# Attention scores of two steps in one run of half-array matmuls, both causal masks behind them

## The reference, cut to what matters

```
# layer 1: 4 memory heads (256 keys, no mask) and 12 heads of causal attention
#          (96 columns of query and key)
# layer 2: 4 memory heads and 12 causal heads with forget gates:
s = einsum('bqhd,bkhd->bhqk', q_i, k) * scale + (F[t] - F[s])
p = softmax(where(key_pos <= q_pos, s, -inf));  out = p @ v
# layer 3: 16 heads of stick breaking
logits = q[:, q0:kend] @ k[:, :kend].T * scale;  mask = ki < qi
log_fail = where(mask, log_sigmoid(-logits), 0)
between = cumsum(log_fail, reverse) - log_fail
w = where(mask, exp(log_sigmoid(logits) + between), 0);  out = w @ v
```

## Time and profile before

| | |
|---|---|
| median of 3 runs | 1189.39 us (1189.06 to 1189.64) |
| profiled execution, its own time | 1190.11 us |
| its span | 1188.4 us |
| granted clock of TensorE | 1.00 over the span |
| PE, PEld busy | 1166.4 and 917.1 us |
| DVE, ACT, POOL busy | 541.3, 604.2, 432.0 us |
| chain that ended last | PE 91% |
| DMA | 84 GB/s over the span |

### The profile page before, as it was taken

How to read it: one execution, slowest core, us unless ns; L and a number is a source line. 1 busy time by engine, 2 the same in 40 slices (tenths; PEclk the granted TensorE clock), 3 DMA queues, 4 the chain that set the end, 5 groups by cost and what they waited for, 6 DMA issues and landing times.

```text
span 1188.4 us, 16087 instructions
## 1 busy us (share of the span) xinstructions
PE 1166.4 (98%) x6031; PEld 917.1 (77%) x6031; DVE 541.3 (46%) x987; ACT 604.2 (51%) x1266; POOL 432.0 (36%) x267
## 2 busy tenths in 40 slices
PE   8999999899999999999999999999999999999998
PEld 7988866578988666668888987887666677888886
DVE  5311475645110655454467556512777750033333
ACT  7444677755353655565545653634655553243242
POOL 6534721134244222214353332444222223444451
PEclk9999999999999999999999999999999999999999
DMA  8533211113335322212332312233222113232321
GB/s 300 144 106 69 65 23 47 54 58 87 99 97 141 91 72 71 72 37 74 106 89 56 123 54 71 84 87 101 67 54 54 54 54 89 88 106 90 104 91 71
DMA packets 111572, 100.98 MB, mean 85 GB/s; under 512 B 21168, under 2 KB 98300, under 8 KB 111496
## 3 DMA queue, kind: packets, MB, share of 16 engines
q1 hardware_dynamic: 108952, 95.38, 27.6%
q0 software_dynamic: 864, 3.15, 0.7%
q10 hardware_dynamic: 1680, 1.44, 0.5%
HBM read 97.83 MB, written 2.12 MB: 84 GB/s over the span
## 4 chain that ended last, share of the span: by engine, by line
PE 91%; DVE 3%; ACT 3%; issue 2%; POOL 1%; DMA 0%; DVEq 0%; ACTq 0%
PE bank L607 50%; PE bank L2019 8%; PE bank L1712 7%; PE bank L1504 6%; PE bank L912 3%; PE bank L878 3%; PE bank L896 2%; PE bank L2035 2%; PE bank L2050 2%; PE bank L2062 2%; PE bank L1296 1%; PE bank L1801 1%; PE bank L717 1%; PE bank L1311 1%; DVE arena L1003 1%
## 5 line engine op out<-in xcount | busy, mean ns | idle before, releaser
L526 POOL TENSOR_TENSOR w_lo<-w_raw,w_hi 128x1024 fp32r<-128x1024 f32 (+4 forms) x157 | 354.5, 2259 | 681.8 <-ACT w_hi L511 681.8
L511 ACT ACTIVATE w_hi<-w_raw 128x1024 fp32r<-128x1024 f32 (+6 forms) x161 | 159.1, 989 | 227.7 <-PE bank L607 203.6
L607 PE MATMUL bank<-acts_hi,w_hi 128*128 128x512 f32 (+1 forms) x576 | 224.0, 389 | 1.0 <-POOL w_lo L526 1.0
L607 PE MATMUL bank<-acts_lo,w_hi 128*128 128x512 f32 (+1 forms) x576 | 222.5, 386 | 0.0
L607 PE MATMUL bank<-acts_hi,w_lo 128*128 128x512 f32 (+1 forms) x576 | 222.5, 386 | 0.0
L607 PEld LDWEIGHTS bank<-acts_hi,w_hi 128*128 128x128 f32 x576 | 108.2, 188 | 24.3 <-POOL w_lo L526 1.5
L607 PEld LDWEIGHTS bank<-acts_lo,w_hi 128*128 128x128 f32 x576 | 108.2, 188 | 22.0
L607 PEld LDWEIGHTS bank<-acts_hi,w_lo 128*128 128x128 f32 x576 | 108.2, 188 | 21.2
L2156 DVE TENSOR_TENSOR_SCAN arena_end<-arena 128x512 f32<-128x512 f32 (+3 forms) x64 | 83.8, 1310 | 59.9 <-ACT arena L2107 59.9
L607 PE MATMUL bank<-w_hi,acts_hi 128*128 128x512 f32 (+4 forms) x240 | 86.9, 362 | 0.2
L607 PE MATMUL bank<-w_hi,acts_lo 128*128 128x512 f32 (+4 forms) x240 | 86.2, 359 | 0.0
(11 more groups left out here) (307 smaller groups left out, 2125.5 us busy)
## 6 DMA issues: line engine op xcount, KB each, us to landing
w_raw<-in_w_in SPq DMA_DIRECT2D x64, 512.0 KB, 3.7
w_raw<-in_w_out SPq DMA_DIRECT2D x24, 512.0 KB, 3.6
w_raw<-in_w_in_b SPq DMA_DIRECT2D x22, 512.0 KB, 3.9
w_raw<-in_w_in_a SPq DMA_DIRECT2D x10, 512.0 KB, 3.8
w_raw<-in_w_mem_kv SPq DMA_DIRECT2D x8, 512.0 KB, 8.0
w_raw<-in_w_sb_proj SPq DMA_DIRECT2D x8, 512.0 KB, 3.4
w_raw<-in_w_ssd_proj SPq DMA_DIRECT2D x8, 512.0 KB, 3.4
arena_shared<-f_kept_rows SPq DMA_DIRECT2D x11, 256.0 KB, 4.5
```

Source lines behind the costliest of these rows:

```text
L511: nc.scalar.activation(w_at(p)[0][:, 0:size], w_raw[p % RAW][:, 0:size], ACT.Copy).then_inc(w_high.sem, 1)
L526: nc.gpsimd.tensor_tensor(lo[:, 0:size], w_raw[p % RAW][:, 0:size], hi[:, 0:size].bitcast(F32), ALU.subtract).then_inc(w_rest.sem, 1)
L607: mm = nc.tensor.matmul(bank_of(S, s, g)[0:lhs.shape[1], 0:rhs.shape[1]], lhs, rhs, start=j + kk + t == 0, stop=j == len(S.pieces) - 1 and ...
```

## The change

`score(s)` is cut in two, `products(s)` and `masks(s)`. In the memory pairs, in attB's causal pairs and in the stick sweep an even step now issues the products of steps s and s+1, then the masks of both; an odd step issues none. `products(s+1)` keeps its own wait for the banks of step s-1, which so comes half a pair of steps earlier in TensorE's program, and the signal of a causal step s is given by its mask, behind the products of step s+1. The full-array causal pairs of attA stay as they were.

The projection's matmuls are dealt out anew, so that pieces of 24 end at odd steps. In attB the first eight steps have 72 instead of 58; then steps have 10 and 14 in turn, and from step 26 on none (before: from 27). In the stick sweep 72 instead of 58 go ahead of step 0, and the last six steps have 4, 4, 5, 5, 6, 0 where they had 14, 6, 6, 6, 6, 0. ScalarE's `collect` and `split` move with them to odd steps.

```
+            def score(s):
+                if s >= steps:
+                    return
+                X = A.item(2 * s)[1]
+                if X.causal and not X.less:
+                    products(s)
+                    masks(s)
+                elif s % 2 == 0:
+                    products(s)
+                    products(s + 1)
+                    masks(s)
+                    masks(s + 1)
...
-                    return (0, 16, 8, 8, 8, 8, 5, 5)[s]
-                if s < 4 * (MP + B_H // 2 - 1) - 1:
-                    return (14, 10, 14, 10)[s % 4]
+                    return (0, 16, 8, 8, 8, 8, 12, 12)[s]
+                if s < 4 * (MP + B_H // 2 - 1) - 2:
+                    return (10, 14)[s % 2]
                 return 0
...
-            ended_at = {2: 0, 5: 1}
-            ended_at.update((4 * MP + 2 * n, 2 + n) for n in range(S.n - 2))
+            ended_at = {2: 0, 5: 1, 4 * MP - 1: 2}
+            ended_at.update((4 * MP + 2 * n + 1, 3 + n) for n in range(S.n - 3))
...
             def score(s):
+                if s < STEPS and s % 2 == 0:
+                    products(s)
+                    products(s + 1)
+                    masks(s)
+                    masks(s + 1)
...
-            turn_in(48 + 10)
+            turn_in(72)
             for s in range(STEPS + 2):
                 score(s)
                 if s % 4 == 2:
                     values(s // 4 - 1)
                 turn_w(2 * s - 4)
                 turn_w(2 * s - 3)
-                if s > STEPS - 4:
-                    turn_in(6 * (s <= STEPS))
+                if s > STEPS - 5:
+                    turn_in((4, 4, 5, 5, 6, 0)[s - STEPS + 4])
                 else:
-                    turn_in((14, 10, 14, 10)[s % 4])
+                    turn_in((10, 14)[s % 2])
...
             split(1)
+            collect(2)
+            split(2)
             for s in range(STEPS + 2):
...
-                if s % 2 == 0 and s < STEPS - 2 or s == STEPS:
-                    q = 2 * PAIRS + 1 if s == STEPS else 2 * p + 2 + s % 4 // 2
+                if s % 2 and s < STEPS - 4 or s == STEPS:
+                    q = 2 * PAIRS + 1 if s == STEPS else 2 * p + 3 + s % 4 // 2
```

More of the change, by code:

```diff
@@ L861, in sweep_pe, with products @@
             steps = len(A.steps)
-            def score(s):
-                if s >= steps:
-                    return
+            def products(s):
                 p, X, b, _, blocks = A.item(2 * s)
@@ L883, in score, with masks @@
                                      start=False, stop=False)
+                if not X.causal:
+                    mm.then_inc(A.scored.sem, 1)
+            def masks(s):
+                _, X, _, _, blocks = A.item(2 * s)
+                n = blocks * P
                 for e in range(2) if X.causal else ():
@@ L886, in score @@
                                           start=False, stop=True)
-                mm.then_inc(A.scored.sem, 1)
+                if X.causal:
+                    mm.then_inc(A.scored.sem, 1)
+            def score(s):
[10 more added lines that the diff above has]
+                    masks(s + 1)
             def turn_w(i):
@@ L2023, in turn_in, with products @@
                     done[0] += 1
-            def score(s):
-                if s >= STEPS:
-                    return
+            def products(s):
                 p, b, _, n = item(2 * s)
@@ L2036, in score, with masks @@
                                      s_kT[p % 2][rows, 0:n], start=True, stop=False)
+            def masks(s):
+                _, _, _, n = item(2 * s)
                 for e in range(2):
```

## The result

| | before | after |
|---|---|---|
| median of the runs, us | 1189.34 (1189.05 to 1189.64, 7 runs) | 1193.63 (1193.31 to 1193.98, 7 runs) |
| span of the profiled execution, us | 1188.4 | 1191.9 |
| granted clock | 1.00 | 1.00 |
| ratio after/before | | 1.0036, interval 1.0026 to 1.0046 |

A forecast was written before the change was run, and what follows sets the result against it. TensorE, busy for 98% of the span, was taken as the bound. Gains of 0.5 (attA memory steps), 0.75 (attB memory steps), 3.8 (rest of attB) and 3.8 (stick sweep) sum to 8.8: 1189.4 becomes 1180.6 us, range 1177.8 to 1185.

The forecast's parts named there:

- the price of an excursion: Switching TensorE to half-array matmuls costs 0.30 us above its columns in a causal step, 0.35 in a memory step.
- 0.31 for a causal pair: Merging two half-array excursions into one saves 0.31 us per causal pair of steps in attB and the stick sweep.
- The rival in which a load is exposed inside the run: Odd step's weight loads can't hide, each run pays 0.11 us, 3.9 of the gain lost: 1184.5 us; chance 0.08.
- Collect and split move ... costed at nothing: ScalarE's collect and split move to odd steps at no cost; without the run's cover, 0.4 us a piece.
- still no wait ... Steady pairs keep 0.31: attB's steady part: even with GpSimd's hold, banks free at 7.6 against 8.3 us, so pairs keep their 0.31 gain.
- I am wrong if: Failure signs: line 878 or 2035 waits in the steady part, or four masks cost more than 0.26 us.
- The memory steps of attA: Gain of 0.5 us: 0.7 from steps 0 to 3, -0.2 from steps 4 to 7 through new waits.
- attB's memory steps: Gain of 0.75 us: 1.05 less 0.3 for products waiting on exponentials.
- attB's end: From step 26 to the next stage: 16.6 us against 17.6 without the change, 1.0 gained.
- The rival on the slower side: Early bank wait stalls every pair, 0.6 us each in attB and the stick sweep: 1197 us; chance 0.07.
- chains take the gain of attA and attB: VectorE's and ScalarE's waits there become real, only the stick sweep gains: 1185 us; chance 0.10.
- The stick sweep's two ends: Late VectorE takes back 0.9 us at the end and 0.3 at the start, leaving the sweep 3.8 gained.

The follow-up runs named there:

- e5: Kernel before the change with only the stick sweep's part of the change (runs, 72 fillers ahead, collects at odd steps): 1185.77 us.
- e10: Changed kernel; in attB only GpSimd waits, starting its subtraction after VectorE's two looks at the next even step's scores, ScalarE's split unmoved: 1186.19 us.
- e3: Changed kernel with ScalarE's two copies of turned weights put between the two exponentials in attB's causal even steps: 1185.38 us.
- e2: Changed kernel with scores issued step by step as before, keeping the moved fillers, collects and splits: 1198.26 us.
- e1: Changed kernel keeping the two-step runs, with fillers, collects and splits put back as in the kernel before: 1198.64 us.
- e8: e6 with attB's last piece of filler spread over steps 24 to 26 (8, 8, 8 matmuls), collected at step 26: 1184.79 us.
- e6: e3 plus the same order of copies, between the two items' sigmoids, in step 28 of the stick sweep: 1185.32 us.
- e9: e6 with attB's first piece ended at step 1 instead of step 2 (counts 0, 24, 6, 6, 6, 6, 12, 12): 1186.14 us.
- e7: e3 with ScalarE's split also one step later in attB from step 7 on, collect unmoved: 1186.41 us over 10 runs.

## Why the prediction was wrong

**Right: the price of an excursion and what hides.** 0.31 for a causal pair was 0.30 to 0.35 in every pair without a wait, and the run to its masks took the forecast 1.28. The rival in which a load is exposed inside the run wanted 1.39, and no run showed it. The rule of the Trainium skill that spoke for that rival ("TensorE: Matmul & The Clock Gate", Part 3) is so not borne out by this trace: the second step's loads, to the row groups of the first (866.41 and 866.84), cost no time. That the price belongs to the half array can be seen in attA of the kernel before: the four full-array matmuls of a step of 128 columns start 0.23 behind the projection matmul (163.97, 164.20), not 0.32, and the masks come 0.44 later (164.64). A step of 512 columns takes 1.72 there (159.87 to 161.59), so 3.33 ns a column, and 0.43 for 128: next to nothing is left above the columns. The stick sweep gave 4.66 + 0.18 - 0.99 = 3.85 for 3.8, and alone, in e5, 3.7.

**Wrong: "Collect and split move ... costed at nothing" and "still no wait ... Steady pairs keep 0.31" in attB.** This step failed, and it is 9.8 of the 12.3 us between forecast and span (+7.0 for -2.8). The prediction saw that GpSimd's subtraction would fall on the pair's first stretch and that one of VectorE's operations could be held 1.6 to 2 us; it was held 1.5 longer. It then asked only whether the banks of the scores would be free at the next run (7.6 against 8.3) and whether the weights would be there. Both were. It did not ask who else stands behind the held operation: look, exponential, and, behind the exponential in ScalarE's program and with no need of it, two copies that free the banks of TensorE's next transposes, which TensorE wants at about 4.5 of the pair's 8.2 us. e10 shows that the hold is the cause of 1.5 of the 1.97 us, e3 that the queue order makes all of it cost, e2 that the wait comes without any run. The other 0.5 is a term that the prediction left out as well: the filler that moved out of the even step had covered ScalarE's copies (e1 against e10 speaks for it; it was not run alone). Neither sign under "I am wrong if" would have caught this: one watched the products (lines 878 and 2035), the other the masks, and the wait came at the transposes.

**Wrong in the rest of attB and attA.** The memory steps of attA gave nothing for 0.5. The first two pairs of steps are shorter by 0.41 and 0.22, but two waits of 0.35 and 0.54 in the last take it back, the second on the same pair of lines again. TensorE's timeline, changed kernel:

```profile
157.92 0.68 PE L917 MATMUL bank<-ident,arena 128*128 128x128 f32 x4 [0.54 <-ACT arena L984]
```

The forecast had this kind of wait at one place, and at L877. attB's memory steps gave +0.15 for -0.75: the run of steps 2 and 3 takes 1.44 to its transposes where the columns ask for 1.06, as `products(3)` has to wait for a bank (ScalarE's second exponential of step 1 is at 389.50, inside the run), and the first piece's collect is waited for 0.3, the uncovered case of e1, since this piece still ends at an even step. attB's end gave +1.09 for -1.0. TensorE's timeline there, changed kernel:

```profile
516.75 0.70 PE L877 MATMUL bank<-arena 64*128 64x256 f32 x4 [1.07 <-DVE stat L1011]
...
521.82 0.30 PE L917 MATMUL bank<-ident,arena 128*128 128x128 f32 x1 [0.85 <-ACT arena L984]
...
523.59 0.48 PE L1067 MATMUL bank<-w_hi,acts_hi 128*128 128x512 f32 x1
```

The forecast had 8.9 from the run of step 26 to item 56's share and 7.7 from there to the next stage; they are 10.1 (504.91 to 514.99) and 8.6. The sum over VectorE's work left out that the products of step 31 (516.75) want a bank that VectorE frees, and that the copies and transposes behind it then come one by one. e8 took back 0.5 of it.

**The rival on the slower side** was right that a hold by GpSimd is the trigger and wrong about the place: it put the wait at `products(s+1)`, in both sweeps, from the hold hitting twice (1197). In attB the view of waits has L877 once, at the end, and a single hold was enough.

**The rival "chains take the gain of attA and attB"**, at 1185, is where the repaired kernels come out (1184.8 to 1186.4), for a part of its reason: steps 8 to 25 have their 2.8 in e3, and the ends and memory steps, where VectorE and ScalarE are behind, give it back.

**The stick sweep's two ends** came out as a sum, not each: the forecast had a loss of 0.3 at either, and they are a gain of 0.18 at the start and a loss of 0.99 at the end. VectorE sets that end, as the forecast said, and e6 shows it.

**Open.** What an earlier first piece is worth in attB's memory steps (e9), how much of attB's end can be had with the copies amid only where no `values` stands ahead of them, and why e7's runs fall in two groups. A kernel in which GpSimd's subtraction is gone from attB altogether was not tried.

## What to carry to other kernels

When a change moves a signal, list every queue in which something stands behind the instructions that it releases, also what has no need of them: an in-order engine passes a delay on to work that was ready long ago. Where one engine can hold another, find out on which operation the hold falls before and after, as the same hold cost nothing in the middle of a pair or beside `values`, and 1.5 us at the start of a short pair. An order of the queue that takes one wait away can make another: e3's copies, put ahead of an exponential, made it wait for `values`. And if a change takes work out from between two others, price what that work was hiding: the runs by themselves made the kernel slower by 9.3 us.

## What the runs showed of the hardware

GpSimd's subtraction of 128x1024, from SBUF to SBUF, lets a share of VectorE (a tensor_scalar, SBUF to SBUF) finish only when it is itself done: 0.14 us behind its end in the changed kernel (433.74 + 2.40 against 434.43 + 1.85), 0.15 in e3, 0.28 in e10, 0.08 in the kernel before. So a share of 0.35 takes 1.85 and one of 0.49 takes 2.63, by where it meets the subtraction. The look that reads a PSUM bank took 0.69 at 433.62 and 0.68 at 436.20, but the first had begun 0.12 ahead of the subtraction, so it doesn't tell whether such a look would be held. The Trainium skill says this of the port that VectorE and GpSimd share ("SBUF — State Buffer", Who interferes with whom): in its two-port modes a tensor_scalar waits for the whole of a GpSimd instruction that began first. This trace agrees; no view shows in which mode a share ran.
